# A hybrid decoder step: another order of work at three seams and in the last unit

## The chip, the cores and the metric

The kernel runs on one core of a Trainium2 chip. The metric is the device time of one execution in microseconds (us). Lower is better.

## What is computed

One inference step of a two-layer trunk on 520 tokens (512 of a prompt, 8 single decode tokens), width 1024, in float32.

```python
# layer 0: sliding-window attention; layer 1: state-space mixer and a gate
u = h.reshape(n, l, 64, 16)
bu = einsum('nlgc,gpc->nlgp', u, bb)            # complex, 64 states a group
_, x = associative_scan(a, bu)                  # over time, from the given state
y = real(einsum('nlgp,gcp->nlgc', x, c)) + d_skip * h
zz = gelu(y) @ w_glu
out = zz[..., :D] * sigmoid(zz[..., D:])        # the gate
# after each mixer: a gated FFN with a causal convolution of width 3
up = rmsnorm(x) @ w_up
c = conv_b + sum_j conv_w[j] * padded_up[:, j:j+l]
x = x + (silu(g) * v) @ w_down                  # g, v = split(c)
```

## The kernel before, in words

Activations lie transposed: 128 channels of a tile on the partitions, 520 tokens in the free dimension, 8 tiles (`KT`). Every dense product is a sequence of *units*: one unit makes one tile of 128 output channels. Float32 is made of two parts, so a unit runs, for each of its 8 (or 11) input tiles and each half of 260 tokens, three matmuls: high weights by high input (L1652), high by low (L1653), low by high (L1654). Two PSUM accumulators and two weight buffers alternate (`b` = 0, 1). `split` makes the two parts of a weight tile: ScalarE (ACT) writes `w_hi` (L781), then VectorE (DVE) writes `w_lo` (L1110). A unit waits for `lo_done` (its weights) and `evac` (its accumulator has been read). The stages in order are qkv, wo, up00, dn00, up01, dn01, the state-space part, glu, up10, dn10, up11, dn11. Each engine's order is written out by hand.

The seams that the change touches:

*Normalised stages up00 and up10.* The first unit runs on unscaled input. After it TensorE (PE) makes the sum of squares (`norm_stat`, L1672), ACT takes the square root (`norm_sd`, L811), DVE the reciprocal (L1129), and DVE multiplies it in when it evacuates the unit (`up_row`, L1480). The third unit needs the first unit's accumulator. On ACT the order is `split` for the third unit, then `norm_sd`; on DVE it is `split`, then the reciprocal.

*The gate (`glu`).* After an even unit (b = 0) DVE runs `split` for the unit two ahead and then copies the accumulator (`glu_in`, L1610). After an odd unit ACT runs `split` and then a tanh (L1087); DVE runs its `split`, makes `glu_out` (L1615), adds it to `x` (L1618, L1619), and both engines then prepare that tile for the next norm: ACT the square and `hx_hi`, DVE the sum `sqs` (L1120) and `hx_lo` (L1123). PE's first unit of up10 waits tile by tile for `hx_lo`.

*The state-space prologue and loop.* Time is cut in 64 chunks of 8 steps; 32 group pairs are handled four at a time in `NJ` = 8 rounds j. From DRAM come tables (`wst`), rotations (`rots`, two DMAs a round), output tables (`recs`) and, by gathers from `h_scr`, the input `u_in` in 8 tiles. PE's pieces:

- `responses(j)` (L1967), 16 matmuls, reads the tables of round j; `turn_responses(h)` (L1976) transposes four results, after which DVE's `responses_out(h)` (L1544) makes the source of half h of a block matrix `toep`, which SP's DMAs spread out (8 DMAs a half, L478).
- `turn_tables(j)` (L1955), 8 transposes, in two alternating PSUM places, copied back to `wst` by `weights_out` (before: one half by ACT, the other by DVE for j below 5).
- `step_stat` makes the norm's statistic; ACT takes the root, DVE the reciprocal `rstd_u`. Then `scale_u(k)` (L1530 on DVE, L744 on POOL for k = 3, 4) scales tile k of `u_in` and releases it.
- `states_in(j)` (L1994) needs tile j scaled, its turned table, and `v_used`, which says that DVE has read the earlier round's states.
- `table_outputs(j)` (L2015) needs `toep`; `state_outputs(j)` (L2029) needs `recs` and POOL's `x_done`; it increments `y_mm`. `turn_outputs(j)` (L2040) needs ACT's `yc` and, for j of 1 and more, DVE's `z_part(j - 1)`.

DVE's round j is: wait for `v_done` and the round's rotations `e_in`, rotate (L1581 to L1586), update the decode states (L1589, releases `v_used`), from j = 3 on `z_part(j - 3)`, two scans (L1596, release `z_done`), then a `scale_u`. POOL then rotates back (L761 to L766) into `x_done`.

PE's order in the main loop is, for j from 3: `states_in(j)`, `turn_outputs(j-3)`, `table_outputs(j-2)`, `state_outputs(j-2)`.

*The end.* After the last unit of dn11, DVE adds 520 columns to `x` (L1449) and SP stores the tile `yT` in one DMA of 260 KB.

Of the kernel before, what the change touches and what calls it, by code (L numbers as in the profile page):

```python
# [13 lines left out]
P = 128  # L14
# [60 lines left out]
def trunk_program(nc, i, o):  # L75
    with ExitStack() as ctx:
# [38 lines left out]
        first_out, _ = place("first_out", 1)  # L115
# [183 lines left out]
        BOTH = 5  # L299
# [48 lines left out]
        def _(sp):  # L348
# [93 lines left out]
            for k in range(KT):  # L442
                sp.wait_ge(sem("h_done"), k + 1)
                sp.dma_start(h_scr[k * P:(k + 1) * P, :], tiles(hg, k)).then_inc(sem(f"h_out{k % 2}"), 16)
                if k < 6:
                    load_tile(*(("dn01", 2 + k // 2) if k < 4 else ("glu", 0)), k % 2)
                if k >= 1:
                    u_tile(k - 1)
            def load_rots(j):

                if j >= ROTS:
                    sp.wait_ge(sem("x_done"), j - ROTS + 1)
                for r in range(2):
                    sp.dma_start(rots[j % ROTS][r][:], e_scr[j][:, r * JQ * NC:(r + 1) * JQ * NC]
                                 ).then_inc(sem(f"e_in{j % ROTS}"), 16)
# [7 lines left out]
            u_tile(KT - 1)  # L463
            sp.wait_ge(units_done, BASE["glu"] + 2)
            load_unit("glu", 1)
# [38 lines left out]
            for m in range(KT):  # L504
# [6 lines left out]
        def _(pool):  # L511
# [220 lines left out]
            for h in range(2):  # L732
                pool.memset(toep[:, h * CH * 512:(h + 1) * CH * 512], 0.0).then_inc(sem("toep_zeroed"), 1)
                if h == 0:
                    u_tile(KT - 1)
# [4 lines left out]
            for k in (3, 4):  # L740
                pool.wait_ge(sem(f"u_in{k}"), 16 * SPG)
                pool.wait_ge(sem(f"u_late{k}"), 16 * (CH + 2 - SPG))
                v = u3[:, CH * k:CH * (k + 1), :]
                pool.tensor_tensor(v, v, rstd_u[:].rearrange("p (o c) -> p o c", o=1).to_broadcast([P, CH, UW]),  # L744
                                   ALU.mult).then_inc(sem("u_ready_late"), 1)
# [30 lines left out]
        def _(act):  # L776
# [36 lines left out]
            def stage(name, work, begin=0):  # L813

                n = INFO[name][3] // 2
                kt = INFO[name][4]
                nxt = ORDER.index(name) + 1
                k_next = STAGES[nxt][4] if nxt < len(STAGES) else None

                def body(it, k):  # L820
                    for b in range(2):
                        u = BASE[name] + 2 * it + b
                        waits_norm = name in NORM_OF and isinstance(it, int) and it == 0 and b == 0
                        if k and name != "dn01":
# [3 lines left out]
                        work(it, b, u)  # L828
# [12 lines left out]
            act.activation(first_out[:], eps[:], ACT.Square)  # L841
# [182 lines left out]
            def weights_out(j):  # L1024

                act.wait_ge(sem("g_turned"), j + 1)
                n = 1 if j < BOTH else 2
                act.activation(wst[:, j * 1024:j * 1024 + n * 512].rearrange("p (b n) -> p b n", b=n),
                               ps[:, turn_bank(j):turn_bank(j) + n, :], ACT.Copy).then_inc(sem("wst_act"), 1)
# [67 lines left out]
        def _(dve):  # L1097
# [34 lines left out]
            def stage(name, take, work=None, begin=0):  # L1132
# [6 lines left out]
                def body(it, k):  # L1139
                    for b in range(2):  # L1140
# [7 lines left out]
                        if k and not waits_norm and name != "dn01":  # L1148
                            split(u + 2, b, k)
                        if work:  # L1150
# [294 lines left out]
            def residual(name, n=None):  # L1445
                def take(it, b, u):
                    m = 2 * it + b
                    dve.wait_ge(units_done, u + 3)
# [76 lines left out]
            def scale_u(k):  # L1525

                dve.wait_ge(sem(f"u_in{k}"), 16 * SPG)
                dve.wait_ge(sem(f"u_late{k}"), 16 * (CH + 2 - SPG))
# [3 lines left out]

            def weights_out(j):

                dve.wait_ge(sem("g_turned"), j + 1)
                dve.tensor_copy(wst[:, j * 1024 + 512:(j + 1) * 1024],
                                ps[:, turn_bank(j) + 1, :]).then_inc(sem("wst_dve"), 1)
# [8 lines left out]
            for j in range(BOTH):  # L1546
                weights_out(j)
                if j == 2:
                    dve.wait_ge(sd_done, 3)
                    dve.reciprocal(rstd_u[:], rstd2).then_inc(rstd_done, 1)  # L1550
                    dve.wait_ge(rstd_done, 3)
                    dve.sem_inc(sem("rstd_u_done"), 1)
                    dve.memset(sq[0][:, 0:2 * JQ * NC].rearrange("p (q c) -> p q c", q=2 * JQ)[:, :, 0:1], 0.0
                               ).then_inc(sem("decay_zeroed"), 1)
                if j == 3:
                    scale_u(0)
                if j == 4:
                    responses_out(0)
            scale_u(1)
            def z_part(j):  # L1560
# [10 lines left out]
            for j in range(NJ):  # L1571
# [30 lines left out]
                if j < 4:  # L1602
                    scale_u(j + 4 if j else 2)
# [3 lines left out]
            def glu(it, b, u):  # L1607
                dve.wait_ge(units_done, u + 3)
                if b == 0:
                    dve.tensor_copy(halves(glu_in[0][:]), acc(0)).then_inc(evac, 1)  # L1610
                    dve.wait_ge(evac, u + 3)
                else:
# [6 lines left out]
                    stt(xd, glu_out[:, SEQ:TOK], 0.5, xd, ALU.mult, ALU.add).then_inc(sem("glu_done"), 1)  # L1619
                    dve.wait_ge(sem("glu_done"), it + 1)  # L1620
# [8 lines left out]
        def _(pe):  # L1629
# [45 lines left out]

            def rest(name, hi, lo):

                with pe.Fori(1, INFO[name][3] // 2) as n:
                    for b in range(2):
                        unit(name, n, b, hi, lo)  # L1680

# [262 lines left out]
            def turn_tables(j):  # L1944
# [4 lines left out]
                if j >= 2:  # L1949
                    pe.wait_ge(sem("wst_act"), j - 1)  # L1950
                    pe.wait_ge(sem("wst_dve"), min(j - 1, BOTH))
# [27 lines left out]
            def states_in(j):  # L1979
                if j in (3, 4):  # L1980
                    pe.wait_ge(sem("u_ready_late"), j - 2)
                else:
                    pe.wait_ge(sem("u_ready"), j + 1 if j < 3 else j - 1)
                pe.wait_ge(sem("wst_act"), NJ if j == 2 else j + 1)
                pe.wait_ge(sem("wst_dve"), min(j + 1, BOTH))
# [16 lines left out]
            def table_outputs(j):  # L2002
                if j == 0:
                    pe.wait_ge(sem("wst_act"), NJ - 1)
# [39 lines left out]
            for j in range(NJ):  # L2044
                responses(j)
                turn_tables(j)
                if j == 1:
                    step_stat()
                if j == 4:
# [114 lines left out]
```

## Time and profile before

| | |
|---|---|
| three runs | 1124.5, 1125.48 (median), 1127.06 us |
| the profiled execution, its own time | 1127.98 us |
| its span, first to last instruction | 1126.2 us (1.78 us lie around it) |
| PE busy | 1106.1 us |
| DVE, ACT, POOL busy | 719.4, 456.8, 427.2 us |
| mean granted clock of PE | 0.995 of full speed |

Times in the trace count from the span's start. A matmul of 260 columns starts 0.12 us after the one before it; its own duration of 0.28 us overlaps the next ones, so a stretch is measured from start to start. The state-space prologue runs from 580.68 to 606.35 us, its loop to 652 us, the gate to 740 us, dn11 to the end.

### The profile page before, as it was taken

What the parts mean: (1) busy time and instruction counts of PE and PEld (TensorE: products, weight loads), DVE (VectorE), ACT (ScalarE), POOL (GpSimd) and SP (SyncE); (2) the same over time, 40 slices, a digit from 0 to 9 for tenths busy, and PEclk for the clock granted to TensorE, in tenths of its full rate; (3) what the DMA queues carried; (4) which work ended last, traced back from release to release, by engine and by line L of the source; (5) the groups of instructions that cost most, each with busy time, mean ns of one, the idle gap of its engine ahead of it and who ended that gap; (6) DMA issues with size and microseconds to landing.
All of it is one profiled execution on the core that took longest, in us unless ns stands there. A gap on an engine that the chain in (4) does not pass through costs nothing. (4 is left out here: it accounts for less than half of the span.)

```text
span 1126.2 us, 25277 instructions
## 1 busy us (share of the span) xinstructions
PE 1106.1 (98%) x9783; PEld 1081.0 (96%) x9783; DVE 719.4 (64%) x1133; ACT 456.8 (41%) x755; POOL 427.2 (38%) x693
## 2 busy tenths in 40 slices
PE   8999999999999999999998999999999999999998
PEld 8997799999999999999997999989999999999998
DVE  6877756798872368876448745567777335777622
ACT  6437853444441144444443323344444113444410
POOL 5114039999999899970458800000000000000000
PEclk9999999999999999999999999999999999999999
DMA  8321003333353233256658322223223322222332
GB/s 290 130 76 49 2 26 125 132 131 130 113 195 121 75 131 109 104 186 236 174 121 242 119 87 86 90 75 101 89 90 115 104 64 93 93 93 93 103 99 94
DMA packets 47704, 129.06 MB, mean 115 GB/s; under 512 B 12064, under 2 KB 17424, under 8 KB 47648
## 3 DMA queue, kind: packets, MB, share of 16 engines
q1 hardware_dynamic: 42272, 114.68, 31.0%
q0 software_dynamic: 5376, 13.63, 3.7%
q8 instruction: 36, 0.59, 0.2%
q14 instruction: 20, 0.16, 0.0%
HBM read 109.79 MB, written 18.21 MB: 114 GB/s over the span
## 5 line engine op out<-in xcount | busy, mean ns | idle before, releaser
L1652 PE MATMUL ps<-hx_hi,w_hi 128*128 128x260 f32 x1600 | 454.3, 284 | 5.2 <-DVE w_lo L1110 1.9
L1654 PE MATMUL ps<-hx_hi,w_lo 128*128 128x260 f32 x1600 | 452.6, 283 | 0.0
L1653 PE MATMUL ps<-hx_lo,w_hi 128*128 128x260 f32 x1600 | 451.2, 282 | 0.0
L781 ACT ACTIVATE w_hi<-w_raw 128x1024 fp32r<-128x1024 f32 (+1 forms) x156 | 175.6, 1126 | 432.3 <-PE ps L1654 432.0
L1652 PEld LDWEIGHTS ps<-hx_hi,w_hi 128*128 128x128 f32 x1600 | 301.6, 189 | 7.9 <-DVE w_lo L1110 2.6
L1653 PEld LDWEIGHTS ps<-hx_lo,w_hi 128*128 128x128 f32 x1600 | 301.5, 188 | 0.1
L1654 PEld LDWEIGHTS ps<-hx_hi,w_lo 128*128 128x128 f32 x1600 | 301.6, 188 | 0.0
L1110 DVE TENSOR_TENSOR w_lo<-w_raw,w_hi 128x1024 fp32r<-128x1024 f32 (+1 forms) x156 | 208.4, 1337 | 94.6 <-ACT w_hi L781 93.9
L1652 PE MATMUL ps<-hid_hi,w_hi 128*128 128x260 f32 x704 | 199.1, 283 | 0.2 <-DVE hid_lo L1471 0.2
L1653 PE MATMUL ps<-hid_lo,w_hi 128*128 128x260 f32 x704 | 198.8, 282 | 0.0
L1654 PE MATMUL ps<-hid_hi,w_lo 128*128 128x260 f32 x704 | 198.7, 282 | 0.0
L1652 PEld LDWEIGHTS ps<-hid_hi,w_hi 128*128 128x128 f32 x704 | 132.5, 188 | 0.4 <-DVE hid_lo L1471 0.4
L1654 PEld LDWEIGHTS ps<-hid_hi,w_lo 128*128 128x128 f32 x704 | 132.5, 188 | 0.0
L1653 PEld LDWEIGHTS ps<-hid_lo,w_hi 128*128 128x128 f32 x704 | 132.3, 188 | 0.0
L1449 DVE TENSOR_TENSOR x<-ps,x 128x520 f32 (+1 forms) x40 | 28.0, 699 | 137.8 <-PE ps L1654 137.8
L1480 DVE TENSOR_TENSOR up_row<-ps,rstd 128x520 f32<-128x520 f32 x88 | 61.5, 699 | 80.0 <-PE ps L1654 79.6
L1488 DVE SCALAR_TENSOR_TENSOR conv<-up_row,cw,conv 128x512 f32<-128x512 f32 x88 | 72.8, 828 | 2.6 <-ACT conv L998 2.5
L1652 PE MATMUL ps<-z_hi,w_hi 128*128 128x260 f32 x256 | 72.8, 284 | 0.1
L1654 PE MATMUL ps<-z_hi,w_lo 128*128 128x260 f32 x256 | 72.3, 283 | 0.0
L998 ACT ACTIVATE conv<-up_row,cb,cw 128x520 f32<-128x520 f32 x88 | 71.8, 816 | 0.8
L1653 PE MATMUL ps<-z_lo,w_hi 128*128 128x260 f32 x256 | 72.1, 282 | 0.0
L1492 DVE SCALAR_TENSOR_TENSOR conv<-up_row,cw,conv 128x512 f32<-128x512 f32 x88 | 68.5, 779 | 3.0
(298 smaller groups left out, 1590.4 us busy)
## 6 DMA issues: line engine op xcount, KB each, us to landing
w_raw<-in_wup SPq DMA_DIRECT2D x88, 512.0 KB, 3.2
w_raw<-in_wdn SPq DMA_DIRECT2D x32, 704.0 KB, 4.1
w_raw<-in_wglu SPq DMA_DIRECT2D x16, 512.0 KB, 3.3
w_raw<-in_wqkv SPq DMA_DIRECT2D x12, 512.0 KB, 3.6
w_raw<-in_wo SPq DMA_DIRECT2D x8, 512.0 KB, 3.6
g_scr<-rec POOLq DMA_DIRECT2D x8, 512.0 KB, 3.2
c_scr<-rec POOLq DMA_DIRECT2D x8, 512.0 KB, 3.2
wst<-g_scr SPq DMA_DIRECT2D x8, 512.0 KB, 7.6
```

Of the source, the lines that this page charges most:

```text
L781: act.activation(w_hi[b][:, 0:kt * P], w_raw[b][:, 0:kt * P], ACT.Copy).then_inc(hi_done, 1)
L998: act.activation(conv[b][:], up_row[b][:, 2:UCOL], ACT.Identity, scale=cw[:, bass.ds(t * 3 + 2, 1)], bias=cb[:, bass.ds(t, 1)]).then_inc(c ...
L1110: dve.tensor_tensor(w_lo[b][:, 0:kt * P], w_raw[b][:, 0:kt * P], w_hi[b][:, 0:kt * P].bitcast(F32), ALU.subtract).then_inc(lo_done, 1)
L1449: tt(halves(tiles(x, m)), acc(b), halves(tiles(x, m)), ALU.add).then_inc(evac, 1)
L1480: tt(halves(up_row[b][:, 2:UCOL]), acc(b), halves(rstd[:]), ALU.mult).then_inc(evac, 1)
L1488: stt(c[:, 0:SEQ], up_row[b][:, 0:SEQ], cw[:, bass.ds(t * 3, 1)], c[:, 0:SEQ], ALU.mult, ALU.add).then_inc(conv_part, 1)
L1492: stt(c[:, 0:SEQ], up_row[b][:, 1:1 + SEQ], cw[:, bass.ds(t * 3 + 1, 1)], c[:, 0:SEQ], ALU.mult, ALU.add).then_inc(conv_done, 1)
L1652: pe.matmul(out, wh, xh, start=(k == 0), stop=False)
L1653: pe.matmul(out, wh, xl, start=False, stop=False)
L1654: ins = pe.matmul(out, wl, xh, start=False, stop=(k == kt - 1))
```

## The change

Five things are edited.

1. *Square-root table early.* In up00 and up10 ACT runs a one-column Sqrt into `first_out` ahead of its `split`; the real one stays where it was.
2. *Gate order.* In `glu` ACT's tanh and DVE's copy, `glu_out` and the additions to `x` come ahead of `split`; the norm's work stays behind it.
3. *Last unit in halves.* The last unit of dn11 runs all its matmuls for tokens 0 to 259, then those for 260 to 519. DVE adds and SP stores each half by itself. As many matmuls as before.
4. *State-space prologue.* PE's order is new (below). ACT alone copies all turned tables. DVE has no copies and scales all eight tiles of `u_in`, tiles 3 and 4 in round 1. POOL scales none.
5. *SP's and POOL's queues.* The last tile of `u_in` is gathered wholly by SP, after the first half of `toep`; POOL clears the second half of `toep` at once. `load_recs(2)` is issued ahead of the second half of `toep`; `load_rots(4)`, the weights of the gate's second pair of units (2 DMAs of 512 KB) and `load_rots(5)` behind it.

```diff
@@ SP
-            u_tile(KT - 1)
             sp.wait_ge(units_done, BASE["glu"] + 2)
-            load_unit("glu", 1)
...
                 if h == 0:
                     load_rots(2)
                     load_recs(1)
+                    sp.wait_ge(sem(f"h_out{(KT - 1) % 2}"), 16 * (KT // 2))
+                    for s in range(CH):
+                        gather(sp, KT - 1, s).then_inc(sem(f"u_in{KT - 1}"), 16)
+                    g = slice(CH * (KT - 1), CH * KT)
+                    sp.dma_start(u3[0:GC, g, 0:NS], h3[:, g, SEQ:TOK]).then_inc(sem(f"u_in{KT - 1}"), 16)
+                    sp.dma_start(u3[P - GC:P, g, NS + NC:UW], h3[:, g, SEQ:TOK]).then_inc(sem(f"u_in{KT - 1}"), 16)
                     load_rots(3)
-                    load_rots(4)
-            for j in range(2, NJ):
+                    load_recs(2)
+            load_rots(4)
+            load_unit("glu", 1)
+            load_rots(5)
+            for j in range(3, NJ):
                 load_recs(j)
...
+            last = tiles(x, KT - 1)
+            sp.wait_ge(sem("y_half"), 1)
+            store(o["yT"][D - P:D, 0:HALF], last[:, 0:HALF])
+            sp.wait_ge(evac, BASE["dn11"] + KT + 2)
+            store(o["yT"][D - P:D, HALF:TOK], last[:, HALF:TOK])
@@ ACT
+                        if waits_norm and name != "qkv":
+                            act.activation(first_out[:, 1 + int(name[2]):2 + int(name[2])], eps[:], ACT.Sqrt)
...
+            responses_out(0)
+            norm_sd(2)
             for j in range(NJ):
                 weights_out(j)
-                if j == 1:
-                    norm_sd(2)
-                if j == 3:
-                    responses_out(0)
-                if j == BOTH - 1:
-                    decays(0)
-                    decays(1)
-            responses_out(1)
+                if j < 2:
+                    decays(j)
+                if j == 0:
+                    responses_out(1)
...
-            def glu(it, b, u):
+            def glu(it, b, u, k):
                 if b == 1:
                     act.wait_ge(units_done, u + 3)
                     act.wait_ge(evac, u + 2)
                     act.activation(halves(glu_in[1][:]), acc(1), ACT.Tanh, scale=0.5).then_inc(sem("tanh_done"), 1)
+                split(u + 2, b, k)
+                if b == 1:
                     act.wait_ge(sem("glu_done"), it + 1)
@@ DVE
+                    if name == "dn11" and isinstance(it, int) and b == 1:
+                        for h in range(2):
+                            if h == 0:
+                                dve.wait_ge(sem("half_done"), 1)
+                            else:
+                                dve.wait_ge(units_done, u + 3)
+                            xh = x[:, m * TOK + h * HALF:m * TOK + (h + 1) * HALF]
+                            tt(xh, acc(b)[:, h], xh, ALU.add).then_inc(sem("y_half") if h == 0 else evac, 1)
+                        return
...
+            scale_u(0)
+            responses_out(0)
             scale_u(1)
+            scale_u(2)
...
                 if j == 1:
                     responses_out(1)
-                if j < 4:
-                    scale_u(j + 4 if j else 2)
+                    scale_u(3)
+                    scale_u(4)
+                elif 2 <= j < 5:
+                    scale_u(j + 3)
@@ PE
-            for j in range(NJ):
-                responses(j)
-                turn_tables(j)
-                if j == 1:
-                    step_stat()
-                if j == 4:
-                    turn_responses(0)
-                    states_in(0)
-                if j == 6:
-                    states_in(1)
+            for j in range(5):
+                responses(j)
+            step_stat()
+            turn_responses(0)
+            turn_tables(0)
+            for j in range(5, NJ):
+                responses(j)
+            turn_tables(1)
+            states_in(0)
+            turn_responses(1)
+            turn_tables(2)
+            turn_tables(3)
+            turn_tables(4)
+            states_in(1)
+            for j in range(5, NJ):
+                turn_tables(j)
+            table_outputs(0)
             states_in(2)
-            turn_responses(1)
-            table_outputs(0)
             state_outputs(0)
```

## Rows read from the trace of the kernel before

**Rows 1.** The page's first part: busy us (share) x instructions.

```profile
PE 1106.1 (98%) x9783; PEld 1081.0 (96%) x9783; DVE 719.4 (64%) x1133; ACT 456.8 (41%) x755; POOL 427.2 (38%) x693
```

**Rows 2.** Waits of PE at the norm seams: total, times, longest.

```profile
PE ps L1652 <- DVE up_row L1480: 1.6, 2, 0.8
PE ps L1652 <- DVE hx_lo L1123: 1.5, 1, 1.5
```

**Rows 3.** Windows: the state-space prologue; length, each engine busy, PE clock, DMA.

```profile
580.70:606.35 25.65, 20.90 (x317) 17.32 (x317) 18.71 (x32) 13.20 (x20) 19.66 (x18) 0.93 0.74 206
```

**Rows 4.** Timeline of PE, state-space part: start, us, instruction, idle before and releaser.

```profile
580.68 0.65 PE L1967 MATMUL ps<-wst,ccd 128*32 128x128 f32 x16
581.25 1.09 PE L1955 MATMUL ps<-ident,wst 128*128 128x128 f32 x8
...
599.42 1.22 PE L1994 MATMUL ps<-u_in,wst 128*64 128x72 f32 x32 [3.59 <-DVE ah L1589]
...
606.35 1.91 PE L2015 MATMUL ps<-toep,u_in 128*72 128x128 f32 x16
...
611.34 0.72 PE L2040 MATMUL ps<-ident,yc 72*128 72x72 f32 x8
...
622.79 0.69 PE L2040 MATMUL ps<-ident,yc 72*128 72x72 f32 x8 [0.37 <-DVE z_lo L1567]
```

**Rows 5.** Timeline of DVE, state-space part; L1581 begins rounds 0, 1, 2 and 4.

```profile
596.68 0.42 DVE L1581 TENSOR_TENSOR vtmp<-ps,rot 128x256 f32<-128x256 f32 x1 [2.34 <-DMA rot<-e_scr]
...
601.23 0.42 DVE L1581 TENSOR_TENSOR vtmp<-ps,rot 128x256 f32<-128x256 f32 x1
...
606.61 0.69 DVE L1544 TENSOR_TENSOR sqs<-ps,skip_d 128x512 f32<-128x512 f32 x1 [0.80 <-DVE zst L1596]
...
607.95 0.42 DVE L1581 TENSOR_TENSOR vtmp<-ps,rot 128x256 f32<-128x256 f32 x1
...
619.38 0.42 DVE L1581 TENSOR_TENSOR vtmp<-ps,rot 128x256 f32<-128x256 f32 x1
```

**Rows 6.** Timeline of SP: the second half of toep, 8 DMAs issued.

```profile
607.33 5.83 SPq L478 DMA_DIRECT2D toep<-sqs  x8
```

**Rows 7.** Tile rot, all 16 DMAs, from issue.

```profile
DMA to landing us min/median/max: 3.0/4.5/7.1
```

**Rows 8.** Tile recs, all 8 DMAs, from issue.

```profile
DMA to landing us min/median/max: 3.2/4.6/8.5
```

**Rows 9.** Line L1530, scale_u on DVE: ns min/median/max, first and last start.

```profile
L1530 DVE TENSOR_TENSOR u_in<-u_in,rstd_u x6: 815/824/2041, 590.1 to 618.6; 128x640 f32<-128x640 f32 x6
```

**Rows 10.** Timeline of ACT: the gate's last unit, and up10's root.

```profile
740.10 1.06 ACT L781 ACTIVATE w_hi<-w_raw 128x1024 fp32r<-128x1024 f32 x1 [4.68 <-PE ps L1654]
741.06 0.59 ACT L1087 ACTIVATE glu_in<-ps 128x520 f32<-128x520 f32 x1
...
748.74 1.28 ACT L811 ACT_TABLE_LOAD   x1
```

**Rows 11.** Timeline of DVE: the gate's first and last units, up10's first, the end.

```profile
658.63 0.69 DVE L1610 COPY glu_in<-ps 128x520 f32<-128x520 f32 x1
...
742.40 0.69 DVE L1615 SCALAR_TENSOR_TENSOR glu_out<-glu_in,glu_in 128x520 f32<-128x520 f32 x1
...
745.13 0.70 DVE L1120 TENSOR_TENSOR sqs<-sqs,sq 128x520 f32<-128x520 f32 x1 [0.76 <-DVE x L1619]
...
748.82 1.23 DVE L1110 TENSOR_TENSOR w_lo<-w_raw,w_hi 128x1024 fp32r<-128x1024 f32 x1 [2.30 <-ACT w_hi L781]
750.76 3.40 DVE L1129 RECIPROCAL rstd<-sq 128x520 f32<-128x520 f32 x1 [0.71 <-ACT sq L811]
...
1122.96 0.70 DVE L1449 TENSOR_TENSOR x<-ps,x 128x520 f32<-128x520 f32 x1 [7.21 <-PE ps L1654]
```

**Rows 12.** The page's sixth part: weight loads, KB each, us to landing.

```profile
w_raw<-in_wup SPq DMA_DIRECT2D x88, 512.0 KB, 3.2
w_raw<-in_wdn SPq DMA_DIRECT2D x32, 704.0 KB, 4.1
```

More of the change, by code:

```diff
@@ L113, in trunk_program @@
         cur[0] += 4 * (GROUPS * UW + 2 * GP * XW)
-        first_out, _ = place("first_out", 1)
+        first_out, _ = place("first_out", 4)
         qkvT, _ = place("qkvT", 12 * TOK, at=D1)
@@ L503, in _ @@
             conv_out(1)
-            for m in range(KT):
+            for m in range(KT - 1):
                 sp.wait_ge(evac, BASE["dn11"] + m + 3)
                 store(o["yT"][m * P:(m + 1) * P, :], tiles(x, m))
+            last = tiles(x, KT - 1)
[3 more added lines that the diff above has]
+            store(o["yT"][D - P:D, HALF:TOK], last[:, HALF:TOK])
             sp.wait_ge(out_done, n_out[0])
@@ L823, in body @@
                         waits_norm = name in NORM_OF and isinstance(it, int) and it == 0 and b == 0
-                        if k and name != "dn01":
+                        if waits_norm and name != "qkv":
+                            act.activation(first_out[:, 1 + int(name[2]):2 + int(name[2])], eps[:], ACT.Sqrt)
+                        if k and name not in ("dn01", "glu"):
                             split(u + 2, b, k)
@@ L827, in body @@
                             norm_sd(NORM_OF[name])
-                        work(it, b, u)
+                        if name == "glu":
+                            work(it, b, u, k)
+                        else:
+                            work(it, b, u)
                         if k and name == "dn01":
@@ L840, in _ @@
             act.wait_ge(sem("eps_set"), 1)
-            act.activation(first_out[:], eps[:], ACT.Square)
+            act.activation(first_out[:, 0:1], eps[:], ACT.Square)
             act.wait_ge(sem("gains_in"), 16)
@@ L1147, in body @@
                             take(it, b, u)
-                        if k and not waits_norm and name != "dn01":
+                        if k and not waits_norm and name not in ("dn01", "glu"):
                             split(u + 2, b, k)
-                        if work:
+                        if name == "glu":
+                            work(it, b, u, k)
+                        elif work:
                             work(it, b, u)
@@ L1544, in responses_out @@
                 tt(rsb[h][:, 0:512], ps[:, 6 + h, :], skip_d[h][:], ALU.add).then_inc(sem("rsb_full"), 1)
[L1546 to L1556, printed above, removed]
-                if j == 4:
-                    responses_out(0)
+            dve.wait_ge(sd_done, 3)
+            dve.reciprocal(rstd_u[:], rstd2).then_inc(rstd_done, 1)
+            dve.wait_ge(rstd_done, 3)
+            dve.sem_inc(sem("rstd_u_done"), 1)
+            dve.memset(sq[0][:, 0:2 * JQ * NC].rearrange("p (q c) -> p q c", q=2 * JQ)[:, :, 0:1], 0.0
+                       ).then_inc(sem("decay_zeroed"), 1)
+            scale_u(0)
+            responses_out(0)
             scale_u(1)
+            scale_u(2)
             def z_part(j):
@@ L1610, in glu @@
                     dve.tensor_copy(halves(glu_in[0][:]), acc(0)).then_inc(evac, 1)
+                    split(u + 2, b, k)
                     dve.wait_ge(evac, u + 3)
@@ L1619, in glu @@
                     stt(xd, glu_out[:, SEQ:TOK], 0.5, xd, ALU.mult, ALU.add).then_inc(sem("glu_done"), 1)
+                    split(u + 2, b, k)
                     dve.wait_ge(sem("glu_done"), it + 1)
@@ L1674, in norm_stat, with last_unit @@
                 ins.then_inc(stat_done, 1)
+            def last_unit(name, hi, lo):
+                n, kt = INFO[name][3] // 2 - 1, INFO[name][4]
+                pe.wait_ge(lo_done, BASE[name] + 2 * n + 4)
+                pe.wait_ge(evac, BASE[name] + 2 * n + 2)
+                for h in range(2):
+                    out = acc(1)[:, h]
+                    for k in range(kt):
+                        wh, wl = w_hi[1][:, k * P:(k + 1) * P], w_lo[1][:, k * P:(k + 1) * P]
+                        c0 = k * TOK + h * HALF
+                        xh, xl = hi[:, c0:c0 + HALF], lo[:, c0:c0 + HALF]
+                        pe.matmul(out, wh, xh, start=(k == 0), stop=False)
+                        pe.matmul(out, wh, xl, start=False, stop=False)
+                        ins = pe.matmul(out, wl, xh, start=False, stop=(k == kt - 1))
+                    ins.then_inc(units_done if h else sem("half_done"), 1)
             def rest(name, hi, lo):
-                with pe.Fori(1, INFO[name][3] // 2) as n:
+                n_end = INFO[name][3] // 2
+                with pe.Fori(1, n_end - (name == "dn11")) as n:
                     for b in range(2):
                         unit(name, n, b, hi, lo)
+                if name == "dn11":
+                    unit(name, n_end - 1, 0, hi, lo)
+                    last_unit(name, hi, lo)
             def two_units(name, hi, lo, k0, ready, lead):
```

40 lines of the change are left out of this document (11 added, 29 removed).

## Prediction

> **What bounds the kernel now.** I read the page's first part: PE is busy for 1106.1 of 1126.2 us [rows 1], so no engine can be swapped for another; what can be won is the 20 us in which PE does not start matmuls. The waits of PE say where it lies, the timelines why. Three places belong to this change. In the state-space prologue PE is busy for 20.90 of 25.65 us, at a mean granted clock of 0.93 [rows 3]: 4.75 us of idle time, and a part at the lower of the two clocks, 1.2 GHz. The biggest wait is the 3.59 us before `states_in(1)`: it waits for round 0 of DVE [rows 4], and DVE waited for the rotations' DMA until 596.68 [rows 5]. At the norm seams PE waits twice 0.8 us for the evacuation and once 1.5 us for `hx_lo` [rows 2]. At the end, DVE's last instruction is done at 1123.66 [rows 11], and the span ends 2.54 us later, with the store alone. The rest of PE's idle time lies in the attention part and at the start, which the change leaves alone.
>
> **1. Prologue.** The order of PE has the same pieces. From start to start `responses` takes 0.57 and `turn_tables` 1.02 (its 1.09 less the same overlap of 0.07), `states_in` 1.15 [rows 4]; `turn_responses`, half as many transposes, 0.5. The clock cost: 0.07 of 25.65 us is 1.8 us of full speed, part of it over idle time; I take 1.3. So a prologue without stalls is 4.75 + 1.3 = 6.05 us shorter.
>
> Does the new order stall? I lay it out on the old time axis, start 580.68.
> - *Round 0.* Its table, states and scaled tile are ready at about 591.4 on PE (five and three responses, statistic, two tables, one turned response, `states_in(0)`). The rotations are now issued without the gate's 1 MB and the last gather ahead of them, at about 586.3 and 586.8 (an estimate: the last `h_scr` store leaves at 583.5, five gathers of 0.47 follow); with 3.0 to 4.5 us [rows 7] they land at 589.8 to 591.3, ahead of need; even the longest, 7.1, costs 2.4. The 3.59 us wait is gone.
> - *`states_in(1)`.* Before, PE reached it at 599.42 - 3.66 = 595.76 [rows 4]. Now one more `responses` and one more `turn_responses` (+1.07) and two `turn_tables` less (-2.04) precede it, plus about 0.15 for a table copy that ACT now makes alone: 594.95, done at 596.1. DVE has finished round 0 by then, so its round 1 starts at 596.3 instead of 601.23 [rows 5]: 4.9 earlier.
> - *The copies on ACT.* One copy per table on ACT against 1.02 of transposing on PE, two PSUM places. ACT's rate equals PE's, so each hand-over can cost 0.1 or so: 0.3 for the whole. DVE loses five copies, and this lets the scaled tiles 0 to 2 be ready before their rounds.
> - *First outputs.* `table_outputs(0)` now precedes `states_in(2)`: 606.35 - 6.05 + 0.3 - 1.15 = 599.45. `toep`'s first half is issued from about 589, when the response is scaled, for 5.9 us as in [rows 6], and lands by 598 to 599: just hidden. The first `turn_outputs` comes at 611.34 - 5.75 = 605.6, and `y_mm` 1 at 604.35.
>
> **2. The loop: where the stall goes.** DVE's rounds are now late relative to PE. Round 1 loses the 0.80 wait ahead of `responses_out` [rows 5] and gains one `scale_u` (0.82, step 0.73 [rows 9]); round 2 therefore starts at 607.95 - 4.95 = 603.0, round 4 at 619.38 - 4.95 = 614.4. Round 4 gains a `scale_u`, so from round 5 on DVE is only 4.2 earlier, while PE came in 5.75 earlier. `turn_outputs` waits for `z_part`, and [rows 4] show that it was already short by 0.37 at 622.79. So PE falls back, in steps of 0.5 to 0.7 at the second, third and fourth `turn_outputs`, to DVE's 4.2 plus the slack of about 0.1 that it had there: 4.3 of the 6.05 stay. (Step of PE: (622.79 - 611.34 - 0.37) / 2 = 5.54; DVE's with a `scale_u`: (619.38 - 607.95) / 2 = 5.7.)
>
> `load_rots(4)` is the transfer that can be late. SP stands at `load_recs(2)` until `y_mm` 1 (604.45), and behind it are that DMA, the eight of `toep`'s second half (5.83 us [rows 6]), and then the rotations of round 4, at about 610.8 and 611.2. With 3.0, 4.5 and 7.1 us [rows 7] they land at 614.2, 615.7 or 618.3 against a need at 614.4: 0 to 3.9 late. With only `toep` ahead I take 615.0, between the lowest and the median: 0.6 lost. Also in this queue: `toep`'s second half lands near 614 and is wanted near 624; the gate's 1 MB is wanted at 656; `load_rots(5)` (613.0, +7.1 at most = 620.1, wanted 620.6) hidden; `load_recs(3)` (613.5, +4.6 = 618.1, at most +8.5 = 622.0 [rows 8], wanted 620.4) hidden or 1.6 late. The last gather, ten DMAs at 596.4 to 601, is wanted at 620. **Prologue and loop: 4.3 - 0.6 = 3.7**, bounds 0.4 (3.9 late) and 5.75 (DVE does not hold PE back).
>
> Here a rule speaks against the change. In the rows `scale_u` takes 0.82 and once, beside POOL's own scaling, 2.04 [rows 9]. The Trainium skill, page SBUF — State Buffer, section "Who interferes with whom", says that a DVE instruction with two SBUF inputs contends with a GpSimd instruction that reads SBUF. `scale_u` is one, and the two that come from POOL now lie beside POOL's rotations. By the row's median they cost 0.73 each; blocked as that page says, they would cost up to 2.04 each (rival D).
>
> **3. Root table early.** The table load is 1.28 [rows 10] and stood between ACT's `split` and the root. Now it lies between `hx_hi` and the end of the first unit, where ACT is idle. The reciprocal can't gain all of it: DVE's `w_lo` at 748.82 lets the next one start 1.14 later, 749.96, instead of 750.76 [rows 11]: 0.80. PE lost 0.94 there (the 0.8 of [rows 2] and the start of its pipeline), so 0.14 stays. Same for up00. **1.6** (bounds 1.5 and 1.9).
>
> **4. Gate.** First units: the copy at 658.63 stood behind `w_lo`; PE restarted at its end, 0.3 after it was ready. It now runs at once, and `w_lo` still is in time: **0.3**. Last unit: the tanh starts at 740.10 instead of 741.06, so `glu_out` at 740.10 + 0.59 + 0.10 = 740.79 instead of 742.40 [rows 10, 11], 1.61 earlier. Ahead of `sqs` now stands `w_lo` (1.14), where DVE had waited 0.76: 1.61 - 1.14 + 0.76 = **1.2** of the 1.5 (bounds 0.9 and 1.5). In between nothing waits: each `w_lo` has 5.74 us of a unit.
>
> **5. Last unit.** Same matmuls; the first half's work is hidden by the second's 3.96 us. DVE's second half: 256 columns take 0.42 [rows 5] against 0.70: 0.28. The store is 130 instead of 260 KB: by the slope between 512 KB in 3.2 and 704 KB in 4.1 us [rows 12] 0.6, by a fixed time nothing; I take 0.3. **0.6** (bounds 0.2 and 0.9). The Trainium skill, page DMA: Bandwidth & Descriptors, section "Anatomy of one DMA — SWDGE (gpsimd) path", has 2.0 us fixed and bytes / 436e3 on top: 0.3 by it, for another kind of queue.
>
> **Sum:** 3.7 + 1.6 + 0.3 + 1.2 + 0.6 = 7.4 us. The profiled execution took 1127.98 (span 1126.2); it would take 1120.6 (span 1118.8). The median of the runs is 2.5 lower, 1125.48; less 7.4 it is **1118.1**.
>
> **Rivals.**
> A. *DVE doesn't hold PE back.* 5.75 in place of 3.7: 1116.0. For it: POOL and DVE get out of each other's way when they start earlier. Against: the 0.37 wait at 622.79. 0.12.
> B. *The rotations of round 4 (and `recs` of round 3) are late*, as the longest of [rows 7]: 3.9 late, 3.3 more than I have: 1121.4. Against: those 7.1 were in a stretch with DMA at 0.74 mean share and the gate's 1 MB ahead. 0.13.
> C. *The clock drops all the same.* Price 1.3 of the prologue: 1119.4. For it: small matmuls fill this stretch. Against: a mean of 0.93 over 25.65 us is 3.6 us at the half clock, so the same pieces ran at the full one for the other 22, and this order leaves PE no idle time like the 3.59. 0.10.
> D. *DVE and POOL block each other* in round 1: 2 x 1.22 on DVE's chain: 1120.5. 0.10.
> E. *Slower.* One mechanism: SP's single queue behind `y_mm` 1. Every us that round 4's rotations land after 615.0 is a us. It eats the gain of 7.4 at 622.4 and makes the kernel slower by 0.2% (2.25 us) from 624.7: 13.5 us after issue, against 7.1 at most. 0.02.
> The forecast has 0.50; 0.03 is for what I don't see.
>
> **Numbers.** About 0.2% is what a measurement of this kernel tells from no change. A to D all stay above it, so faster 0.93, same 0.05, slower 0.02. The range takes in A, C, D and most of B: 1115.6 to 1121.3.
>
> **What would show it.** In the profile after: no PE wait on `ah` above 0.3 us and a clock of 1.00 in the prologue; prologue's first `turn_outputs` 25 us after its first `responses` (before 30.66); then waits of PE on `z_lo` of 0.5 to 0.7, three in a row, and a DVE wait of about 0.6 on `rot` in round 4; waits on `up_row` near 0.1 and on `hx_lo` near 0.3; the span ends 2 us after DVE's last instruction. I am wrong if PE waits for `toep`, for `wst` by more than 0.5 in sum, or if `recs` is late.

## The result, and the profile after

The changed kernel takes 1119.64 us (median of 5 runs, 1117.88 to 1123.37) against 1125.48 (1124.5 to 1127.51): ratio 0.9946, 95% interval 0.9932 to 0.9959. That is 5.8 us less (4.6 to 7.7). 7.4 were forecast, which the interval still holds, so the traces below have to say whether the forecast missed.

The profiled execution is the slowest of the five: 1123.37 us with a span of 1121.5. The other four have spans of 1116.0 to 1117.8. So its local losses are read beside three more traces of the same kernel (below). The page's first part, beside [rows 1]:

```profile
PE 1106.2 (99%) x9783; PEld 1083.1 (97%) x9783; DVE 713.4 (64%) x1131; ACT 459.6 (41%) x757; POOL 424.6 (38%) x686
```

PE has the same instructions and the same busy time. What changed is when it waits. Its waits at the places of the change (total, times, longest), beside [rows 2]:

```profile
PE ps L2071 <- DVE z_lo L1579: 3.3, 1, 3.3
...
PE ps L2046 <- DMA toep<-sq: 0.9, 1, 0.9
...
PE ps L1990 <- ACT wst L1037: 0.5, 2, 0.2
...
PE ps L1668 <- DVE hx_lo L1132: 0.2, 1, 0.2
```

The waits on `ah` (3.6) and `up_row` (2 x 0.8) are gone, that on `hx_lo` fell from 1.5 to 0.2. A new one of 3.3 on `z_lo` stands in the loop. The timeline of PE through prologue and loop, beside [rows 4]:

```profile
579.09 2.39 PE L2002 MATMUL ps<-wst,ccd 128*32 128x128 f32 x80
...
585.26 1.52 PE L2002 MATMUL ps<-wst,ccd 128*32 128x128 f32 x48
...
592.54 1.22 PE L2025 MATMUL ps<-u_in,wst 128*64 128x72 f32 x32
...
597.90 1.94 PE L2046 MATMUL ps<-toep,u_in 128*72 128x128 f32 x16 [0.91 <-DMA toep<-sq]
...
604.07 0.72 PE L2071 MATMUL ps<-ident,yc 72*128 72x72 f32 x8
...
609.62 0.72 PE L2071 MATMUL ps<-ident,yc 72*128 72x72 f32 x8
...
618.45 1.20 PE L2071 MATMUL ps<-ident,yc 72*128 72x72 f32 x8 [3.31 <-DVE z_lo L1579]
619.43 3.62 PE L2046 MATMUL ps<-toep,u_in 128*72 128x128 f32 x16
622.99 2.59 PE L2060 MATMUL ps<-recs,xst 64*72 64x128 f32 x32
...
649.74 0.67 PE L2071 MATMUL ps<-ident,yc 72*128 72x72 f32 x8
```

The prologue is as long as forecast: from the first `responses` to the first `turn_outputs` 604.07 - 579.09 = 24.98 us (before 30.66). Its window, with PE's clock at 1.00 instead of 0.93 [rows 3]:

```profile
579.10:602.82 23.72, 22.33 (x365) 20.17 (x365) 18.57 (x35) 15.78 (x20) 17.53 (x17) 1.00 0.63 167
```

Then the loop loses it all in this execution. `turn_outputs(2)` waits 3.31 us, and behind the wait it takes 1.20 us instead of 0.70, `table_outputs` 3.62 instead of 1.91, `state_outputs` 2.59 instead of 1.97: 2.8 us more in all. The granted clock is the first number behind the engines in the windows there (0.5 is the lower of the two levels, 1.2 GHz; a window that also holds the full one has a mean between):

```profile
615.00:620.00 5.00, 1.69 (x17) 1.58 (x12) 4.83 (x12) 0.43 (x2) 1.79 (x4) 0.75 0.98 358
620.00:625.00 5.00, 5.00 (x41) 4.68 (x41) 4.90 (x12) 0.64 (x3) 4.73 (x6) 0.57 0.11 41
```

From the first `responses` to the eighth `turn_outputs` it is 649.74 - 579.09 = 70.65 us, before 651.32 - 580.68 = 70.64. I call this stretch the *seam* below. What is late stands in DVE's timeline (rounds 2, 3 and 4 begin at L1593), beside [rows 5]:

```profile
601.04 0.42 DVE L1593 TENSOR_TENSOR vtmp<-ps,rot 128x256 f32<-128x256 f32 x1
...
603.55 1.41 DVE L1608 TENSOR_TENSOR_SCAN zst<-sq,vrot 128x256 f32<-128x256 f32 x2
...
605.74 0.42 DVE L1593 TENSOR_TENSOR vtmp<-ps,rot 128x256 f32<-128x256 f32 x1
...
608.92 2.10 DVE L1608 TENSOR_TENSOR_SCAN zst<-sq,vrot 128x256 f32<-128x256 f32 x2
...
615.03 0.42 DVE L1593 TENSOR_TENSOR vtmp<-ps,rot 128x256 f32<-128x256 f32 x1 [3.15 <-DMA rot<-e_scr]
...
618.22 1.26 DVE L1608 TENSOR_TENSOR_SCAN zst<-sq,vrot 128x256 f32<-128x256 f32 x2
```

and in SP's, where the rotations of round 4 follow `toep`'s second half, as [rows 6]:

```profile
603.35 5.86 SPq L477 DMA_DIRECT2D toep<-sqs  x8
609.25 1.10 SPq L454 DMA_DIRECT2D rot<-e_scr  x2
```

The dense seams, up10's and the end; DVE first, then ACT and PE, beside [rows 10, 11]:

```profile
742.45 0.77 DVE L1132 SCALAR_TENSOR_TENSOR hx_lo<-x,gains,hx_hi 128x520 fp32r<-128x520 f32 x1
...
745.52 1.22 DVE L1119 TENSOR_TENSOR w_lo<-w_raw,w_hi 128x1024 fp32r<-128x1024 f32 x1 [2.28 <-ACT w_hi L786]
746.66 3.39 DVE L1138 RECIPROCAL rstd<-sq 128x520 f32<-128x520 f32 x1
...
1118.84 0.43 DVE L1466 TENSOR_TENSOR x<-ps,x 128x260 f32<-128x260 f32 x1 [3.50 <-PE ps L1705]
```

```profile
742.12 1.28 ACT L830 ACT_TABLE_LOAD   x1
...
745.32 0.68 ACT L816 ACTIVATE sq<-ps,eps 128x520 f32<-128x520 f32 x1
```

The table load lies at 742.12, in ACT's idle time, and the reciprocal follows `w_lo` at once. All that comes after the seam, from the eighth `turn_outputs` to the end of the span, is 1121.5 - 649.74 = 471.8 us against 1126.2 - 651.32 = 474.9: **3.1 us** less (first gate unit, gate's last unit, up10's root, end; forecast 0.3 + 1.2 + 0.8 + 0.6 = 2.9). The end alone: from DVE's last start to the span's end 2.66 instead of 3.24 us, 0.58 less.

### The profile page after: what moved, and what is told of

It is laid out like the page before. It is cut to its first block and busy times, and to the rows that moved or that the text cites. A ratio compares the mean times of both kernels' runs of the same rounds, so it can differ in the third digit from the quotient of the medians.

```text
span 1121.5 us, 25264 instructions
## 1 busy us (share of the span) xinstructions
PE 1106.2 (99%) x9783; PEld 1083.1 (97%) x9783; DVE 713.4 (64%) x1131; ACT 459.6 (41%) x757; POOL 424.6 (38%) x686
## 5 line engine op out<-in xcount | busy, mean ns | idle before, releaser
L1668 PE MATMUL ps<-hid_hi,w_hi 128*128 128x260 f32 x682 | 192.8, 283 | 0.1
L1669 PE MATMUL ps<-hid_lo,w_hi 128*128 128x260 f32 x682 | 192.5, 282 | 0.0
L1670 PE MATMUL ps<-hid_hi,w_lo 128*128 128x260 f32 x682 | 192.5, 282 | 0.0
L1668 PEld LDWEIGHTS ps<-hid_hi,w_hi 128*128 128x128 f32 x682 | 128.4, 188 | 0.3 <-DVE hid_lo L1491 0.3
L1670 PEld LDWEIGHTS ps<-hid_hi,w_lo 128*128 128x128 f32 x682 | 128.3, 188 | 0.0
L1669 PEld LDWEIGHTS ps<-hid_lo,w_hi 128*128 128x128 f32 x682 | 128.2, 188 | 0.0
```

The lines of the kernel that those rows point to most:

```text
L1668: pe.matmul(out, wh, xh, start=(k == 0), stop=False)
L1669: pe.matmul(out, wh, xl, start=False, stop=False)
L1670: ins = pe.matmul(out, wl, xh, start=False, stop=(k == kt - 1))
```

## The experiments

The seam in every trace, in us: from the first `responses` to the first and to the eighth `turn_outputs`, DVE's wait for rotations, PE's main waits, and whether PE ran a stretch of the loop or prologue at the lower clock. The seam is read from one trace of each row. Ratios are of the medians of several executions, against the kernel before beside them (its medians there were 1126.24 to 1126.47 us, and 1125.48 with the first result), with their 95% intervals. The traces of after, e2 and e8 are of executions well above the medians given here (1123.37, 1120.67 and 1121.17 us), so their stalls need not be typical.

| kernel | median us | ratio | to 1st | to 8th | DVE on rot | PE waits | lower clock |
|---|---|---|---|---|---|---|---|
| before (profile above) | 1125.48 | 1 | 30.66 | 70.64 | 2.34 | ah 3.59 | yes |
| before, again | 1126.15 | one execution | 29.22 | 69.12 | 0.66 | ah 1.91 | yes |
| e3_dense_only | 1122.47 | 0.9961 (0.9948 to 0.9975) | 30.00 | 69.88 | 1.44 | ah 2.69 | yes |
| e6: e3, gate's 1 MB last | 1120.57 | 0.9942 (0.9924 to 0.996) | 26.90 | 67.90 | none | wst 1.14, z_lo 0.74, 0.55 | no |
| after | 1119.64 | 0.9946 (0.9932 to 0.9959) | 24.98 | 70.65 | 3.15 | toep 0.91, z_lo 3.31 | yes |
| again | 1120.26 | 0.9946 (0.9925 to 0.9967) | 24.54 | 67.46 | 1.12 | toep 0.47, z_lo 1.72 | yes |
| again_look2 | 1120.06 | one execution | 24.77 | 67.97 | 1.61 | toep 0.70, z_lo 1.97 | yes |
| again_look3 | 1119.74 | one execution | 24.54 | 67.70 | 1.32 | toep 0.47, z_lo 1.92 | yes |
| e2: gate's 1 MB last | 1118.48 | 0.9922 (0.9904 to 0.994) | 25.26 | 68.00 | 3.14 | 1.19, z_lo 3.15 | no |
| e1: rots(4) early | 1119.07 | 0.9927 (0.991 to 0.9943) | 24.51 | 65.83 | none | toep 0.44, z_lo 0.55, recs 1.11 | no |
| e4: both | 1117.91 | 0.9924 (0.991 to 0.9939) | 24.41 | 65.29 | none | toep 0.34, z_lo 0.57, 0.55 | no |
| e5: e4, scale 3 in round 0 | 1117.92 | 0.9919 (0.9905 to 0.9934) | 24.74 | 65.40 | none | toep 0.67, z_lo 0.45, 0.55 | no |
| e7: e4, POOL scales 3, 4 | 1117.91 | 0.992 (0.9903 to 0.9937) | 24.98 | 65.75 | none | ah 0.98, z_lo 0.56, 0.55 | no |
| e8: e4, scales ahead | 1118.53 | 0.9928 (0.9915 to 0.9942) | 27.45 | 67.10 | none | toep 1.75 | yes |

**The changed kernel again, three more traces.** No edit.

> The changed kernel once more, for a second profile of it. If the late rotations of round 4 are the rule, DVE again waits 2 us or more for rot in round 4, PE again 2 us or more for z_lo at the third turn_outputs, and the time is again some 1119.6 us. If the first profile was an outlier, that wait is below 1 us, and the granted clock stays full in the loop.

> The changed kernel once more, one look. Theory (the landing of round 4's rotations behind toep's second half varies by several us from one execution to the next): DVE's wait on rot in round 4 is anywhere between 0 and 3.5 us (1.12 and 3.15 so far), PE's z_lo wait is this plus 0.2 to 0.6, and the stretch is 65.9 plus the DVE wait plus 0.4 to 1.6 where the clock halves. Rival (it is a fixed delay of the order): again 1.1 or 3.15.

> As the look before, the same kernel and the same expectation: one more value for the wait on rot, for the PE wait that follows it, and for whether the clock halves after it.

The wait on `rot` is there every time, 1.12, 1.61 and 1.32 us; the profile's 3.15 is the longest of the four. The first expectation had two cases, over 2 us or under 1 us at the full clock, and met neither: 1.12 us, and the clock fell. In `again`, DVE and PE:

```profile
612.27 0.42 DVE L1593 TENSOR_TENSOR vtmp<-ps,rot 128x256 f32<-128x256 f32 x1 [1.12 <-DMA rot<-e_scr]
```

```profile
615.69 0.70 PE L2071 MATMUL ps<-ident,yc 72*128 72x72 f32 x8 [1.72 <-DVE z_lo L1579]
616.22 3.50 PE L2046 MATMUL ps<-toep,u_in 128*72 128x128 f32 x16
```

DVE's 1.12 become 1.72 on PE, because DVE was about 0.6 behind already, and the lower clock adds 3.50 - 1.91 = 1.6 us. The seams of these three, 67.5 to 68.0, give the typical one: 67.7.

**e1: the rotations of round 4 ahead of `recs` 2 and `toep`'s second half.**

```diff
                     load_rots(3)
+                    load_rots(4)
                     load_recs(2)
-            load_rots(4)
             load_unit("glu", 1)
```

> load_rots(4) issued right behind load_rots(3), ahead of load_recs(2) and the second half of toep; nothing else differs from the changed kernel. Theory (the transfer is late because of its place in SP's queue): no DVE wait on rot in round 4 (below 0.2 us), no PE wait above 1 us in the loop, full granted clock through the loop, and in place of the 3.3 us wait two or three waits of 0.3 to 0.7 us on z_lo, where DVE is the slower one; 1116.0 to 1118.3 us. Rival (DVE's chain with the added scale_u is the bound anyway): the same time as the changed kernel, 1119.6. Rival (the clock falls in this stretch whatever waits): a half-clock stretch of 3.4 us remains, 1118 to 1119.

**e2: the gate's 1 MB behind the loop's last loads.**

```diff
             load_rots(4)
-            load_unit("glu", 1)
             load_rots(5)
             for j in range(3, NJ):
                 ...
+            load_unit("glu", 1)
             conv_out(0)
```

> The gate's 1 MB of weights goes behind the last rotations and recs of the loop; load_rots(4) keeps its place behind toep's second half. If rots(4) is late by its issue behind y_mm 1 and toep, the DVE wait on rot in round 4 stays at 2 to 3.3 us and the time at 1119 to 1120. If the 1 MB issued right behind it shares the DMA engines with it and makes it late, the wait falls below 1 us and the time to 1116 to 1118.3.

PE in e1, then in e2:

```profile
615.97 0.69 PE L2071 MATMUL ps<-ident,yc 72*128 72x72 f32 x8 [0.55 <-DVE z_lo L1579]
616.50 1.91 PE L2046 MATMUL ps<-toep,u_in 128*72 128x128 f32 x16
619.53 1.97 PE L2060 MATMUL ps<-recs,xst 64*72 64x128 f32 x32 [1.11 <-DMA recs<-c_scr]
```

```profile
618.49 0.69 PE L2071 MATMUL ps<-ident,yc 72*128 72x72 f32 x8 [3.15 <-DVE z_lo L1579]
619.02 1.91 PE L2046 MATMUL ps<-toep,u_in 128*72 128x128 f32 x16
```

The place in the queue behind `toep` is what makes the rotations late: e1 has no wait on them, e2 has one of 3.14 us with the 1 MB out of the way. e1's time, 1119.07, lies above the 1116.0 to 1118.3 that were expected, beside a kernel before of 1126.47; its ratio on 1125.48 gives 1117.3. e2's 1118.48 lies below the 1119 to 1120 of its first case, though the wait is that case's. But the 1 MB delays what stands behind it: with the first stall gone, e1 waits 1.11 us for `recs`. And e2 shows that a stall need not bring the lower clock: behind 3.15 us `table_outputs` took 1.91.

**e4: e1 and e2 together; e5, e7 and e8: DVE's scalings elsewhere.**

```diff
 # e5, against e4
+                if j == 0:
+                    scale_u(3)
-                if j == 1:
+                elif j == 1:
                     responses_out(1)
-                    scale_u(3)
                     scale_u(4)
 # e8, against e5
                     scale_u(4)
-                elif 2 <= j < 5:
-                    scale_u(j + 3)
+                    scale_u(5)
+                elif j < 4:
+                    scale_u(j + 4)
 # e7, against e4: POOL, after clearing toep, and no scale_u(3), scale_u(4) on DVE
+            for k in (3, 4):
+                ...
+                pool.tensor_tensor(v, v, rstd_u[:]..., ALU.mult).then_inc(sem("u_ready_late"), 1)
```

> The order of e1 (rotations of round 4 ahead of recs 2) with the gate's 1 MB moved behind the loop's last loads. Theory (the loop's loss is made by late small transfers in one queue, each with its own cause: rots 4 behind toep, recs 3 behind the gate's 1 MB): the DVE wait on rot stays away, the PE wait of 1.11 us on recs goes too, only the z_lo wait of about 0.55 stays, PE's clock is full in the loop, and the stretch from the first responses to the eighth turn_outputs is 65.83 - 1.1 = 64.7 us; time about 1118.0, ratio 0.992. Rival (the DMA engines' load decides, not the place in the queue): recs or rot is late by about 1 us again, at another round, stretch 65.8 or more, time as e1, 1119.1.

> As e4, and scale_u of tile 3 moves from DVE's round 1 to its round 0, where DVE stood idle for about 1.1 us ahead of round 1. Theory (DVE's rounds hold PE by a small amount at turn_outputs): the z_lo wait of 0.55 goes and the stretch is about 64.2 us, 0.5 less than e4's; time about 0.5 below e4's, within what timing can tell. Rival (DVE's rounds are no bound once the rotations are early): the stretch equals e4's within 0.2.

> As e4, but tiles 3 and 4 are scaled by POOL while it is idle ahead of its first rotation, as in the kernel before; DVE's round 1 is 1.4 to 1.6 us shorter. Theory A (DVE's load in round 1 is what PE meets as the z_lo wait): the z_lo wait is gone, the stretch is 0.5 or more below e4's, at about 64.2. Rival (PE's own pieces are the bound in the loop): stretch as e4's within 0.2, and DVE waits longer for v_done instead. A POOL scaling beside DVE's first scale_u could make one of these 2 us instead of 0.82; it would then delay states_in(0) by about 1.2 us.

> As e4, with DVE's scalings one round ahead: tile 3 in round 0, tiles 4 and 5 in round 1, tile 6 in round 2, tile 7 in round 3, none in round 4. In e4, e5 and e7 alike PE waited 0.45 to 0.57 us twice for z_lo, and DVE's rounds 3 and 4 were 6.05 us apart without any idle time. Theory (PE meets the length of DVE's rounds that hold a z_part, two scans and a scale_u, not the work of rounds 0 and 1): the second of these waits goes and the first stays or shrinks, the stretch from the first responses to the eighth turn_outputs is about 64.8 us against 65.3 to 65.4; time within 0.5 us of e4's 1117.9. Rival (the waits come with PE's own order and return whatever DVE has to do): two waits of 0.5 and a stretch of 65.3. Third case: tile 7's gather has not landed at round 3; a DVE wait on DMA u_in would show it.

e4's time came as expected (1117.91, 1118.0 expected). Its seam is 65.29, only 0.54 under e1's where 1.1 was expected: the 1.11 us on `recs` is gone, but with PE that much earlier a second wait on DVE comes up. PE in e4, and the starts of DVE's rounds 3, 4 and 5:

```profile
614.90 0.69 PE L2071 MATMUL ps<-ident,yc 72*128 72x72 f32 x8 [0.57 <-DVE z_lo L1579]
...
620.94 0.70 PE L2071 MATMUL ps<-ident,yc 72*128 72x72 f32 x8 [0.55 <-DVE z_lo L1579]
```

```profile
605.43 0.42 DVE L1593 TENSOR_TENSOR vtmp<-ps,rot 128x256 f32<-128x256 f32 x1
...
611.48 0.42 DVE L1593 TENSOR_TENSOR vtmp<-ps,rot 128x256 f32<-128x256 f32 x1
...
617.53 0.42 DVE L1593 TENSOR_TENSOR vtmp<-ps,rot 128x256 f32<-128x256 f32 x1
```

DVE's rounds with a `z_part` and a scaling are 6.05 us long and have no idle time (part of it the scans, 2.10 us beside POOL's rotation); PE's step is 609.62 - 604.07 = 5.55. So PE loses 0.5 in each of them. Moving work out of the rounds before does nothing, as the rival said for e5: e5 and e7 have the same two waits, and DVE idles ahead of round 2 instead (1.20 us in e5, 0.94 in e7). e7's seam is still 0.46 longer than e4's, where the rival had it within 0.2. e7 shows what the scaling costs beside POOL's; DVE, then POOL:

```profile
586.70 3.67 DVE L1557 TENSOR_TENSOR u_in<-u_in,rstd_u 128x640 f32<-128x640 f32 x2
```

```profile
585.71 3.98 POOL L755 TENSOR_TENSOR u_in<-u_in,rstd_u 128x640 f32<-128x640 f32 x2
```

Two scalings on DVE take 3.67 us beside POOL's two, 1.55 in e4 with POOL doing none; `states_in(1)` waits 0.98 on `ah` behind it (`states_in(0)`, where the expectation had the delay, waits for nothing). This agrees with the rule that the prediction weighed (the Trainium skill, page SBUF — State Buffer, section "Who interferes with whom").

e8 says less than it was meant to: `toep`'s first half landed late.

```profile
600.10 3.51 PE L2048 MATMUL ps<-toep,u_in 128*72 128x128 f32 x16 [1.75 <-DMA toep<-sq]
```

PE lost 1.75 in the wait and 1.6 at the lower clock, came into the loop that much later, and DVE was in time anyway; that the second `z_lo` wait would go is not shown, and the 64.8 expected was missed by 2.3. What it does show: the DVE round without a scaling ran from 615.48 to 620.78, 5.30 us, under PE's 5.55, and the loop without any wait takes 647.54 - 607.89 = 39.65 us, against 40.88 in e4.

**e3: the old state-space part with the dense edits alone. e6: e3 with one more edit,** the gate's 1 MB behind the loop's last loads.

```diff
             u_tile(KT - 1)
             sp.wait_ge(units_done, BASE["glu"] + 2)
-            load_unit("glu", 1)
             ...
+            load_unit("glu", 1)
             conv_out(0)
```

> The kernel before with the root table early, the gate order and the last unit in halves, without the new prologue and queues. The prediction's terms for these are 1.6 + 1.5 + 0.6 = 3.7 us: 1121.8. The profile after reads 0.85 + 0.83, 0.33 + 1.40 and 0.57 = 4.0: 1121.5. If they are worth less because a stall moves on, 1123 or more, and then the prologue is worth more than 2 us.

> The kernel e3 (old state-space prologue; root table early, gate order, last unit in halves) with one more edit: the gate's 1 MB behind the loop's last loads. Theory 1 (the wait of 2.69 to 3.59 us on ah in the old prologue comes from what stands ahead of the rotations in SP's queue): the wait falls below 1 us, the half clock at 598 to 602 is gone, and the stretch from the first responses to the first turn_outputs falls from 30.0 to about 26.5 us; time 1122.5 - 3 = 1119.5, nearly as good as the whole change. Theory 2 (the order of PE, ACT and DVE made it): the stretch stays at 30.0 to 30.7, time 1122.5.

PE in e3, then in e6, at `states_in(1)` and `states_in(2)`:

```profile
597.64 1.73 PE L2039 MATMUL ps<-u_in,wst 128*64 128x72 f32 x32 [2.69 <-DVE ah L1612]
```

```profile
596.00 1.22 PE L2039 MATMUL ps<-u_in,wst 128*64 128x72 f32 x32 [1.14 <-ACT wst L1038]
...
599.98 1.22 PE L2039 MATMUL ps<-u_in,wst 128*64 128x72 f32 x32 [1.16 <-issue]
```

Two DMAs moved in SP's queue take away the wait on `ah` and the lower clock, and shorten the prologue by 3.1 us (30.00 to 26.90; 26.5 expected). What is left of the new order adds 2.5 (26.90 to 24.41, e4): the order of PE, ACT and DVE, and also the later last gather and POOL's queue, which no run here takes apart. So of the prologue's gain more than half was the queue's.

The times say the same. e3's edits alone gave 4.4 us by its ratio (1122.47 us; 1121.5 to 1121.8 expected). e6 came to 1120.57 (1119.5 expected), a ratio of 0.9942, and the whole change to 0.9946, with seams of 67.90 and 67.7: as submitted, the new order with its late rotations is no better than the old order with two DMAs moved. Only with e1's and e2's edits on top, in e4, does it gain over e6 in the seam, by 2.6 us.

**The kernel before once more.** No edit.

> The kernel before once more, one look. The prediction took the 2.5 us between the profiled execution and the median of the runs as carrying over unchanged. Theory: the state-space part is where executions of the kernel before differ too; an execution near the median waits less than 3.59 us on ah ahead of states_in(1) (2.69 in e3) and its stretch from the first responses to the eighth turn_outputs is 69.5 to 69.9 us in place of 70.64, so that the seam's gain measured on the median is about 2 us and not 2.9. Rival: the stretch is 70.6 again and the 2.5 us lie elsewhere (start, attention).

```profile
597.43 2.12 PE L1994 MATMUL ps<-u_in,wst 128*64 128x72 f32 x32 [1.91 <-DVE ah L1589]
```

Its wait is 1.91 and its seam 69.12, a little under the 69.5 to 69.9 expected. With the 70.64 of [rows 4] and e3's 69.88 the three traces of the old order have a mean of 69.88; the one that the prediction was worked out on had the longest stall. Its span is 1124.4 and its time 1126.15. Of the 1.8 us between the two spans 1.5 lie in the seam.

## Why the forecast was 1.6 us too good

*Dense parts: right.* Forecast 3.7 (1.6 + 0.3 + 1.2 + 0.6). Traces: 3.1 behind the seam, and up00's root about as much as up10's. At up10 the distance from the start of `hx_lo` to the reciprocal fell from 750.76 - 745.75 = 5.01 to 746.66 - 742.45 = 4.21, the 0.80 of the forecast. Together 3.9, and e3 alone measured 4.4 us (2.8 to 5.9).

*Prologue: right in length, in part by luck.* 24.98 against a forecast of 25 (24.54 to 24.77 in the three further traces), no wait on `ah`, full clock, `wst` waits of 2 x 0.24. But one of the three signs of being wrong came true: the "just hidden" `toep` is not quite hidden. PE waits 0.34 to 0.91 for it in seven traces of this order, 1.75 in e8, where it brought the lower clock too; e2 has 1.19 at that place, put down to a copy, and e7 none. A saving that the forecast did not have made up for it: five and three `responses` back to back take 3.8 us from start to start, where 8 x 0.57 = 4.56 were reckoned. Rivals A and D are out: D because the two scalings of round 1, beside POOL's rotation, took 2.11 us together: 0.56 more than the 1.55 that two took with POOL idle, not 2 x 1.22 more; A because DVE does hold PE back once nothing else does. That term was right in size: forecast 5.75 - 4.3 = 1.45 in three waits, measured 1.12 in two (e4). The changed kernel itself never shows them: it has the one wait on `z_lo` instead.

*`load_rots(4)`: late, as forecast, but by more.* Forecast: DVE waits 0.6, at full clock. Measured from the first `responses`: the rotations were to land at 615.0 - 580.68 = 34.3 us and did at 33.9, 34.4 and 34.1 (`again` and the two traces after it; 35.9 in the profile). They were to be wanted at 614.4 - 580.68 = 33.7 and were at 32.8. So the landing was right and the need was wrong by 0.9. 0.4 of it is the start of round 2 (601.04 - 579.09 = 21.95 against 22.3). 0.6 is rounds 2 and 3: I gave them the 11.4 us that they took in the kernel before, and they took 4.70 + 6.14 = 10.84. What was shorter is the pair of scans in round 2, 1.41 us (603.55 above; 1.60 in `again`) against 2.09 before:

```profile
610.46 2.09 DVE L1596 TENSOR_TENSOR_SCAN zst<-sq,vrot 128x256 f32<-128x256 f32 x2
```

Before, POOL was at work all through these scans; now it had finished round 1 and stood idle for the last 0.68 us before it took up round 2's:

```profile
605.04 1.37 POOL L766 TENSOR_TENSOR ptmp<-zst,rot 128x256 f32<-128x256 f32 x1 [0.68 <-DVE zst L1608]
```

DVE's wait became 1.1 to 1.6 in place of 0.6. On PE it shows as one wait of 1.7 to 2.0, the arrears of DVE included. That is no more than the 1.45 + 0.6 = 2.05 forecast for all these waits together: the waiting was about right in sum.

*The clock, the term that was missing.* I put the chance of the lower clock into the prologue (rival C). It came in the loop, behind the very stall that I had forecast, and costs 1.6 us in `again` (3.50 - 1.91) and as much in the two traces after it (`table_outputs` 3.31 and 3.57 us). I had priced that stall at its length alone. Beside e4, whose rotations are early, the late ones cost 2.4 us (65.3 to 67.7), where the forecast had 0.6: 0.6 to 0.85 is more waiting, 1.6 the clock.

*From one profile to the median.* I let the 2.5 us between the profiled execution and the median carry over. 0.76 of it (70.64 - 69.88) is the stall that the change removes, so that much could not be won on the median. In typical traces the seam gained 69.88 - 67.7 = 2.2, where 3.7 was forecast: one half of the miss of 1.5 is this baseline, the other a seam of 67.7 instead of 70.64 - 3.7 = 66.9. 3.9 + 2.2 = 6.1 against a measured 5.8. In the profiled execution the rotations of rival B came true as well (3.15 late; `recs` was not), the seam gained nothing, and its time of 1123.37 lies above the range; the median of 1119.64 lies inside.

*What stays open.* Why those rotations took 5.8 and 5.6 us in two traces (after, e2) and 4.3 to 4.8 in three: all stand behind the same eight DMAs. Why the lower clock comes after one stall and not after another; in the attention part, too, the granted clock from 100 to 105 us was 0.71 in the profile and 1.00 in `again`, in the same kernel. Whether e4 beats the changed kernel in time: the intervals 0.991 to 0.9939 and 0.9932 to 0.9959 just overlap; its seam is 2.2 us shorter than the shortest of the four.

## What to carry to other kernels

Work out when a transfer is wanted in the new order, not only when it lands: an edit that makes the consumer earlier makes the same landing late, and a round gets shorter when the engine beside it is done sooner. When a stall of PE stays in a forecast, add the price of the lower clock behind it as a case of its own: in the state-space part it followed 8 of the 9 stalls of 1.7 to 3.6 us seen here, and cost 1.3 to 2.8 us. Before reordering engines, try moving large, not yet wanted loads behind small urgent ones in the same queue: here that alone took 2.0 of the 4.6 us that the seam gave in all (69.88 to 67.90, to 65.29 in e4), and the gate lost nothing by it (from the eighth `turn_outputs` to the end e4 takes 1115.8 - 644.05 = 471.75 us, the changed kernel 471.8). Take a second trace before pricing a stall: the same wait was 3.59 and 1.91 us in two executions of the kernel before.

## What the runs showed of the hardware

In the state-space part PE fell to its lower clock, 1.2 GHz, behind stalls of 1.72, 1.75, 1.92, 1.97 and 3.31 us (`table_outputs` 3.31 to 3.62 us instead of 1.91), and in the old order behind 1.91, 2.69 and 3.59 us (`states_in(1)` 2.12 and 1.73 instead of 1.22 behind the first two, the next `responses` 1.08 instead of 0.65 behind the third). It did not behind the 3.15 in e2, nor, in this part, behind any of 0.3 to 1.2. The same transfer in the same place of the queue landed 4.3 to 5.8 us after its issue. DVE's pair of scans took 1.26 us where POOL waited, as at 618.22, and 2.10 where it was rotating, as at 608.92.
